# The low parts of the down phases' operands, split between VectorE and GpSimd

## The chip, the cores and the metric

The kernel runs on one core of one Trainium2 chip. The metric is device time of one execution in microseconds (us), lower is better. The engines named below are TensorE (PE in the profile: matmuls; PEld: its weight loads), VectorE (DVE), ScalarE (ACT), GpSimd (POOL) and SyncE (SP, which here issues all DMAs). SBUF is the on-chip memory that they share, PSUM the one that TensorE writes.

## The reference, cut to what matters

One layer over 1024 latent tokens and 256 context tokens, 1024 features wide, all in fp32:

```
x += 1/2 * gate1 * SwiGLU_1(mod(RMSNorm(x)))      # D_FF = 2816, context tokens too
x += gate2 * W_out [ Retention || ChunkGMLP ](mod(RMSNorm(x)) W_in)
x += 1/2 * gate3 * SwiGLU_2(mod(RMSNorm(x)))
return rmsnorm(x, final_g)

def swiglu(h, w1, w2):
    gate, up = jnp.split(h @ w1, 2, axis=-1)
    return (jax.nn.silu(gate) * up) @ w2          # this last product is the "down" one
```

The change is in the last line, the down product of each of the two SwiGLUs for the latent tokens.

## The kernel before

**Operands in two parts.** A matmul in full fp32 is made of three in the type fp32r. ScalarE copies an operand `raw` into fp32r (its high part), another engine computes the low part `raw - high`, and TensorE adds high x high, high x low and low x high in PSUM (L2186, L2187, L2188 for the down product).

**The down phase.** The down product uses Strassen's scheme in Winograd's form: 7 products (`NM`) of half size, each over 11 tiles (`HALF`) of the 2816 hidden features, so 77 steps (`STEPS`). One step has four groups of three matmuls with 512 columns. Its operands are one tile of tokens (128 x 512, gated activations or sums of them) and one of weights (128 x 512), which SyncE loads from HBM into a ring of six slots (`SLOTS`, L274 to L279). A slot is raw[:, 0, :] for tokens and raw[:, 1, :] for weights. Per step, in this order:

- SyncE: `load_step` (L634), as soon as the step six earlier is done on TensorE (`s_step`).
- ScalarE: `ring_high` (L1048), one copy of 128 x 1024, counted by `s_rh`.
- VectorE: `ring_low` (L1620), one subtraction of 128 x 1024, counted by `s_rl`.
- TensorE: `down_step` (L2190) waits for `s_rl`.

Between the steps each engine has further duties at written-out places, given by functions of the step (`mixer_opening` in the first feed-forward, `final_downs`, `final_squares` and `final_sum` in the second): VectorE adds finished products to the stream (`down_added`), sums parts of the modulation (`latent_sums`, L1449), and prepares the context's norm (`norm_mean(1, 0)` behind step 31, `norm_diagonal(1, 0)` behind step 32). TensorE sums that norm's squares behind step 26 and spreads its scale with `norm_scale(1, 0)` behind step 29 (L2006), for which it needs VectorE's diagonal DG (L1326), which needs GpSimd's reciprocal root RS (`norm_rsqrt`, L749).

**GpSimd's order.** Nothing reorders instructions: each engine runs its list as written, and a wait holds up all that stands behind it. Before a down phase stand the 22 blocks of the gate and up products. For the last of them, block 21, `gated_sums` (L778) makes three operations (L786, L788, L795) on the gated activations that VectorE has just finished (L1613, L1618). Behind the first phase's blocks GpSimd has `norm_rsqrt(1, 0)`, the low parts of the mixer's first two weight units (`low(0)`, `low(1)`, L743, 128 x 2048 each), and eight low parts of context tokens (HCL, L846). Behind the second's it has ten additions of squares for the final norm (L906, L911). During the steps it has nothing else to do.

Of the kernel before, what the change touches and what calls it, by code (L numbers as in the profile page):

```python
# [8 lines left out]
ALU = mybir.AluOpType  # L9
# [135 lines left out]
def layer(nc, x, ctx, c2, ada_units, w_units, w2_units, b_ada, norm_g, final_g, decay, ws, bs, cosine, sine, consts, powers, ident, out):  # L145
# [10 lines left out]
    with stack:  # L156
# [214 lines left out]
        s_w2st = sem("down_weight_sums_stored")  # L371
        s_ring = [sem(f"down_operands_loaded{r}") for r in range(NSLOT)]
        s_rh = sem("down_operands_high_done")
        s_rl = sem("down_operands_low_done")
        s_step = sem("down_step_done")
        s_sqt = sem("final_squares_done")
        s_qt = [sem(f"final_squares_added{t}") for t in range(2)]
        s_out = sem("stored")


# [353 lines left out]
        def _(pool):  # L734
# [25 lines left out]
                    pool.tensor_tensor(tokens(hl, b)(k), modulated_tile(place, b, k), tokens(hh, b)(k).bitcast(F32),  # L760
                                       ALU.subtract).then_inc(s_hl, 1)

            def feed_forward(f):
                s_wh, s_wl, s_fp = BS[f].wh, BS[f].wl, BS[f].fp

                def low_part(slot, src, count):
                    pool.wait_ge(s_wh, count)
                    pool.tensor_tensor(WVL[:, slot], src, WVH[:, slot].bitcast(F32), ALU.subtract).then_inc(s_wl, 1)

                def weight_low(g, m, raw=None):  # L770
                    low_part(weight_slot(f, g, m), weight_block(m, raw), weights_done(f, g, m))

                def token_low(v, k):
                    high, low = token_block((3, 2, 4, 5)[v], k)
                    pool.wait_ge(s_vh[v], 4 * f + k + 1)
                    pool.tensor_tensor(low, token_sum(v)[:, k, :], high.bitcast(F32), ALU.subtract).then_inc(s_vl[v], 1)

                def gated_sums(g):  # L778

                    h = HB[g % 2]  # L780
                    first, second = h[:, 0:TB], h[:, TB:SEQ]
                    for t in range(2):
                        pool.wait_ge(s_fp[t], g + 1)
                    if g >= HALF:
                        pool.wait_ge(s_trl, 16 * (HALF * f + g - HALF + 1))
                        pool.tensor_tensor(TBF[:, 0, :], first, TBF[:, 0, :], ALU.subtract).then_inc(s_ts, 1)  # L786
                        pool.wait_ge(s_ts, sums_done(f, g) - 2)
                        pool.tensor_tensor(TBF[:, 1, :], TBF[:, 0, :], TBF[:, 1, :], ALU.add).then_inc(s_ts, 1)  # L788
                        pool.wait_ge(s_ts, sums_done(f, g) - 1)
                    if f or g:  # L790
                        pool.wait_ge(s_tst, sums_stored(f, g - 1))
                    if g < HALF:
                        pool.tensor_tensor(TBF[:, 2, :], first, second, ALU.subtract).then_inc(s_ts, 1)
                    else:
                        pool.tensor_tensor(TBF[:, 2, :], second, TBF[:, 1, :], ALU.subtract).then_inc(s_ts, 1)  # L795

                def weight_pair_sums(j):

                    pool.wait_ge(s_w2, 48 * (HALF * f + j + 1))
                    n = SUMS * f + 4 * j  # L800
                    a11, a21, a12, s3, a22 = (WB[:, i, :] for i in range(5))
                    pool.tensor_tensor(s3, a11, a21, ALU.subtract).then_inc(s_w2s, 1)
                    pool.wait_ge(s_w2s, n + 1)
                    pool.tensor_tensor(a21, a21, a22, ALU.add).then_inc(s_w2s, 1)
                    pool.wait_ge(s_w2s, n + 2)
                    pool.tensor_tensor(a11, a21, a11, ALU.subtract).then_inc(s_w2s, 1)
                    pool.wait_ge(s_w2s, n + 3)
                    pool.tensor_tensor(a12, a12, a11, ALU.subtract).then_inc(s_w2s, 1)

                if f:  # L810
                    for n, slot in enumerate(DIRECT):
                        low_part(slot, direct_block(n), n + 1)
                    for m in ORDER1[:3]:
                        weight_low(1, m, RAW1)
                    norm_rsqrt(2, 2)
                    norm_low(2, 2, 0, 4)
                    pool.wait_ge(s_wl, weights_done(f, 1, 3))
                    for m in ORDER1[5:]:
                        weight_low(1, m, RAW1)
                else:  # L820
                    weight_low(1, 0)
                    pool.wait_ge(s_yb, NF)
                    for m in ORDER[1:]:
                        weight_low(1, m)
                for k in range(4):
                    token_low(3, k)
                for g in range(NF):
                    gated_sums(g)
                    if 1 <= g <= HALF:
                        weight_pair_sums(g - 1)  # L830

            pool.wait_ge(s_negh, 1)
            norm_rsqrt(0, 0)
            norm_low(0, 0)
            norm_rsqrt(0, 1)
            norm_rsqrt(0, 2)
            feed_forward(0)
            norm_rsqrt(1, 0)
            pool.wait_ge(s_w2st, 16 * HALF)
            pool.wait_ge(s_col, ADA_STEPS[0])  # L840
            pool.wait_ge(s_tst, sums_stored(0, NF - 1))
            low(0)
            low(1)
            for k in range(KT):
                pool.wait_ge(s_hh, 8 * J[1, 0] + k + 1)
                pool.tensor_tensor(HCL[:, k, :], XC[:, k, :], HCH[:, k, :].bitcast(F32), ALU.subtract).then_inc(s_hl, 1)  # L846
            norm_rsqrt(1, 1)
            norm_low(1, 1, 0, 4)
            norm_low(1, 1, 4, KT)
# [28 lines left out]
            for n, (i, name, a, b) in enumerate(FILLS):  # L878
# [19 lines left out]
                    norm_rsqrt(2, 1)  # L898
                if (name, a, b) in (("out", 1, 2), ("out", 1, 3)):
                    norm_low(2, 1, 4 * (b - 2), 4 * (b - 1))  # L900
            feed_forward(1)
            for n in range(1, 4):
                pool.wait_ge(s_sqt, n + 1)
                if n > 1:
                    pool.wait_ge(s_qt[1], n - 1)
                pool.tensor_tensor(SQT[1][:, 0, 0:TB], SQT[1][:, 0, 0:TB], SQT[1][:, n, 0:TB], ALU.add).then_inc(s_qt[1], 1)  # L906
            for n in range(1, KT):
                pool.wait_ge(s_sqt, 4 + n + 1)
                if n > 1:
                    pool.wait_ge(s_qt[0], n - 1)  # L910
                pool.tensor_tensor(SQT[0][:, 4, 0:TB], SQT[0][:, 4, 0:TB], SQT[0][:, (4 + n) % KT, 0:TB],  # L911
                                   ALU.add).then_inc(s_qt[0], 1)
            for b in (1, 2):
                norm_rsqrt(3, b)

# [375 lines left out]
        def _(dve):  # L1291
# [266 lines left out]
            def feed_forward(f, at_step):  # L1558
# [61 lines left out]
                def ring_low(s):  # L1620
                    raw, low_part, high_part = SLOTS[s % NSLOT]
                    dve.wait_ge(s_rh, STEPS * f + s + 1)
                    dve.tensor_tensor(low_part, raw, high_part.bitcast(F32), ALU.subtract).then_inc(s_rl, 1)  # L1623

                def block_period(g, q):
                    a = ADA_PERIODS.get(g) if f == 0 else None
# [356 lines left out]
        def _(pe):  # L1983
# [147 lines left out]
            def feed_forward(f, at_step, at_tile):  # L2131
# [58 lines left out]
                def down_step(s):  # L2190
                    i, j = divmod(s, HALF)
                    pe.wait_ge(s_rl, STEPS * f + s + 1)
                    for d in range(4):
                        if j == 0 and i >= 2:
                            pe.wait_ge(s_fyd, 4 * (i - 2) + d + 1)
                        ins = step_tile(s, d)
                    ins.then_inc(s_step, 1)

                def down_product():
                    if f:  # L2200
                        pe.wait_ge(s_xm, 8 * (J[2, 2] + 1))
                    pe.wait_ge(s_fp[1], 1)
                    pe.wait_ge(s_mods, N_ADA if f else ADA_STEPS[0])
                    for s in range(STEPS - MAJOR):
                        if s == HALF:
                            pe.wait_ge(s_c11, NF - 1)
                            pe.wait_ge(s_c12, NF - 1)
                            pe.wait_ge(s_c22, NF - 1)
                            pe.wait_ge(s_g1, NF)
                        if s == 3 * HALF and f == 0:  # L2210
                            pe.wait_ge(s_xm, 8 * (J[1, 0] + 1))
                        down_step(s)
                        at_step(s)
                    for d in range(4):
                        for s in range(STEPS - MAJOR, STEPS):
                            if d == 0:
                                pe.wait_ge(s_rl, STEPS * f + s + 1)
                            ins = step_tile(s, d)
                        ins.then_inc(s_step, 1)
                        at_tile(d)  # L2220
# [189 lines left out]
            def final_sum(s):  # L2410
                if s == STEPS - MAJOR - 1:
                    pe.wait_ge(BS[1].fyd, 24)
                    square_sum(0, 4, (s_qt[0], KT - 1), first=True).then_inc(s_st, 1)

            def final_norm(d):
                if d == 1:
                    norm_scale(3, 1)
                if d == 2:
                    pe.wait_ge(s_ms, J[3, 1] + 1)
                    square_sum(1, 0, (s_qt[1], 3), first=True)  # L2420
                    square_sum(1, 4, (s_sqt, 13))
                if d == 3:
                    for k in range(5, KT):
# [86 lines left out]
```

## Time and profile before

| what | us |
|---|---|
| median of 3 runs (lowest to highest) | 2052.42 (2052.02 to 2053.18) |
| profiled execution | 2052.53 |
| its span | 2050.7 |
| TensorE busy (L2186 to L2188 are the down phases) | 2008.0, 98% |
| VectorE busy | 1266.6, 62% |
| ScalarE busy | 758.9, 37% |
| GpSimd busy | 496.3, 24% |
| low parts of the ring on VectorE (L1623), 154 | 99.7 + 102.7 |

The first down phase begins at 688.5 us of the span, the second at 1821.1. An engine's busy time says how much it works, not whether another waits for it; idle time counts only where TensorE, which is busy almost throughout, waits. A matmul's reported duration (0.39 us) overlaps the next one's, so their pace is read from their starts.

### The profile page before, as it was taken

What the parts mean: (1) busy time and instruction counts of PE and PEld (TensorE: products, weight loads), DVE (VectorE), ACT (ScalarE), POOL (GpSimd) and SP (SyncE); (2) the same over time, 40 slices, a digit from 0 to 9 for tenths busy, and PEclk for the clock granted to TensorE, in tenths of its full rate; (3) what the DMA queues carried; (4) which work ended last, traced back from release to release, by engine and by line L of the source; (5) the groups of instructions that cost most, each with busy time, mean ns of one, the idle gap of its engine ahead of it and who ended that gap; (6) DMA issues with size and microseconds to landing.
All of it is one profiled execution on the core that took longest, in us unless ns stands there. A gap on an engine that the chain in (4) does not pass through costs nothing.

```text
span 2050.7 us, 26021 instructions
## 1 busy us (share of the span) xinstructions
PE 2008.0 (98%) x10112; PEld 1689.4 (82%) x10112; DVE 1266.6 (62%) x1887; ACT 758.9 (37%) x1098; POOL 496.3 (24%) x311
## 2 busy tenths in 40 slices
PE   7999999999999998999999999999999999999997
PEld 5999988888888887888989898877788888888886
DVE  5988666556788678775454324468656555555555
ACT  4333533333333354445121221446333333334342
POOL 1000042333221103014222222554332421210001
PEclk9999999999999999999999999999999999999998
DMA  8964436666656786733101011121656644466664
GB/s 335 353 258 145 143 106 204 214 205 206 215 186 215 256 297 196 258 112 109 42 21 42 31 43 61 62 82 57 212 198 206 213 161 151 161 212 192 191 194 154
DMA packets 108762, 343.52 MB, mean 168 GB/s; under 512 B 11488, under 2 KB 20960, under 8 KB 90464
## 3 DMA queue, kind: packets, MB, share of 16 engines
q1 hardware_dynamic: 108640, 341.85, 49.1%
q8 instruction: 81, 1.33, 0.3%
q14 instruction: 41, 0.34, 0.1%
HBM read 267.36 MB, written 74.45 MB: 167 GB/s over the span
## 4 chain that ended last, share of the span: by engine, by line
PE 85%; issue 5%; DVE 5%; ACT 2%; DMA 1%; POOL 1%; DVEq 0%; POOLq 0%; SPq 0%; ACTq 0%
PE PS L2144 12%; PE PS L2146 12%; PE PS L2145 12%; PE PS L1986 8%; PE PS L1988 8%; PE PS L1987 8%; PE PS L2186 5%; PE PS L2188 5%; PE PS L2187 5%; PE PS L2102 4%; DVE WVL L1577 1%; PE PS L2362 1%; DMA WR<-w_units 1%; PE PS L2043 1%; PE PS L2023 0%
## 5 line engine op out<-in xcount | busy, mean ns | idle before, releaser
L2144 PE MATMUL PS<-HH,WVH 128*128 128x512 f32 x672 | 265.8, 395 | 0.0
L2146 PE MATMUL PS<-HH,WVL 128*128 128x512 f32 x672 | 263.7, 392 | 0.0
L2145 PE MATMUL PS<-HL,WVH 128*128 128x512 f32 x672 | 261.9, 390 | 0.0
L1986 PE MATMUL PS<-HH,WH 128*128 128x512 f32 x416 | 165.0, 397 | 2.9 <-DVE WL L1768 2.9
L1988 PE MATMUL PS<-HH,WL 128*128 128x512 f32 x416 | 162.0, 389 | 0.0
L1987 PE MATMUL PS<-HL,WH 128*128 128x512 f32 x416 | 161.9, 389 | 0.0
L1577 DVE TENSOR_TENSOR WVL<-WR,WVH 128x512 fp32r<-128x512 f32 x160 | 115.1, 720 | 72.3 <-ACT WVH L1004 72.3
L2146 PEld LDWEIGHTS PS<-HH,WVL 128*128 128x128 f32 x672 | 126.1, 188 | 29.9
L2145 PEld LDWEIGHTS PS<-HL,WVH 128*128 128x128 f32 x672 | 126.2, 188 | 27.8
L2144 PEld LDWEIGHTS PS<-HH,WVH 128*128 128x128 f32 x672 | 126.3, 188 | 26.5
L1623 DVE TENSOR_TENSOR DLOW<-DRAW,DHIGH 128x1024 fp32r<-128x1024 f32 x78 | 99.7, 1286 | 71.3 <-ACT DHIGH L1052 70.9
L1623 DVE TENSOR_TENSOR HL<-HLF,HH 128x1024 fp32r<-128x1024 f32 x76 | 102.7, 1361 | 61.1 <-ACT HH L1052 60.6
L1004 ACT ACTIVATE WVH<-WR 128x512 fp32r<-128x512 f32 x164 | 98.1, 623 | 96.2 <-PE PS L2146 80.3
L743 POOL TENSOR_TENSOR WL<-WR,WH 128x2048 fp32r<-128x2048 f32 x20 | 92.2, 4612 | 166.4 <-ACT WH L921 166.4
L1052 ACT ACTIVATE DHIGH<-DRAW 128x1024 fp32r<-128x1024 f32 x78 | 82.5, 1060 | 124.8 <-DMA DRAW<-down_weight_sums 73.8
L2186 PE MATMUL PS<-DHIGH 128*128 128x512 f32 x312 | 124.2, 398 | 0.0
L921 ACT ACTIVATE WH<-WR 128x2048 fp32r<-128x2048 f32 x47 | 89.6, 1906 | 90.0 <-PE PS L1988 90.0
L2187 PE MATMUL PS<-DLOW,DHIGH 128*128 128x512 f32 x312 | 122.7, 393 | 0.0
L2188 PE MATMUL PS<-DHIGH,DLOW 128*128 128x512 f32 x312 | 122.4, 392 | 0.0
L749 POOL TENSOR_TENSOR RS<-MS,NEGH 128x4 f32<-128x4 f32 (+3 forms) x16 | 22.9, 1434 | 404.9 <-DVE MS L1323 347.0
L1004 ACT ACTIVATE WVH<-ST 128x512 fp32r<-128x512 f32 x125 | 78.7, 631 | 111.1 <-PE PS L2146 66.1
L2186 PE MATMUL PS<-HH 128*128 128x512 f32 x304 | 119.4, 393 | 0.1
(282 smaller groups left out, 4974.5 us busy)
## 6 DMA issues: line engine op xcount, KB each, us to landing
WR<-w_units SPq DMA_DIRECT2D x89, 1024.0 KB, 5.8
gated<-HB SPq DMA_DIRECT2D x44, 512.0 KB, 6.6
down_weight_sums<-WB SPq DMA_DIRECT2D x22, 1024.0 KB, 3.8
gated_sums<-TBF SPq DMA_DIRECT2D x22, 768.0 KB, 4.1
AW<-ada_units SPq DMA_DIRECT2D x12, 1024.0 KB, 13.2
HLF<-down_weight_sums SPq DMA_DIRECT2D x46, 256.0 KB, 3.4
W2RB<-w_units SPq DMA_DIRECT2D x22, 512.0 KB, 3.6
WB<-w_units SPq DMA_DIRECT2D x22, 512.0 KB, 3.6
```

Source lines behind the costliest of these rows:

```text
L1004: act.activation(WVH[:, slot], src, ACT.Copy).then_inc(s_wh, 1)
L1577: dve.tensor_tensor(WVL[:, m], weight_block(m), WVH[:, m].bitcast(F32), ALU.subtract).then_inc(s_wl, 1)
L1623: dve.tensor_tensor(low_part, raw, high_part.bitcast(F32), ALU.subtract).then_inc(s_rl, 1)
L1986: pe.matmul(dst, wh, xh, start=first, stop=False)
L1987: pe.matmul(dst, wh, xl, start=False, stop=False)
L1988: return pe.matmul(dst, wl, xh, start=False, stop=last)
L2144: pe.matmul(bank[:, :], wh, xh, start=first, stop=False, skip_group_check=True)
L2145: pe.matmul(bank[:, :], wh, xl, start=False, stop=False, skip_group_check=True)
L2146: ins = pe.matmul(bank[:, :], wl, xh, start=False, stop=k == 3, skip_group_check=True)
L2186: pe.matmul(bank[:, :], wh, xh, start=j == 0 and i in (0, 1, 3), stop=False, skip_group_check=True)
L2187: pe.matmul(bank[:, :], wh, xl, start=False, stop=False, skip_group_check=True)
L2188: return pe.matmul(bank[:, :], wl, xh, start=False, stop=j == HALF - 1, skip_group_check=True)
```

## The change

The low part of a step is made by two engines. VectorE subtracts the tokens' half alone (128 x 512), GpSimd the weights' half (128 x 512, a new semaphore `s_rlw`), and TensorE waits for both. GpSimd's loop over the 77 steps stands behind its loop over the blocks. What GpSimd did behind the blocks is now done at fixed steps: in the first phase `norm_rsqrt(1, 0)` behind step 31, `low(0)` behind 36, `low(1)` behind 40, one context tile behind each of 46 to 53; in the second the additions of squares behind 32 to 34, 65 to 67 and 72 to 75. These additions are counted by one semaphore instead of two.

```diff
         s_rh = sem("down_operands_high_done")
-        s_rl = sem("down_operands_low_done")
+        s_rl = sem("down_tokens_low_done")
+        s_rlw = sem("down_weights_low_done")
...
-            def feed_forward(f):
+            def feed_forward(f, at_step):
...
                     gated_sums(g)
                     if 1 <= g <= HALF:
                         weight_pair_sums(g - 1)
+                for s in range(STEPS):
+                    raw, low_part, high_part = SLOTS[s % NSLOT]
+                    pool.wait_ge(s_rh, STEPS * f + s + 1)
+                    pool.tensor_tensor(low_part[:, 1, :], raw[:, 1, :], high_part[:, 1, :].bitcast(F32),
+                                       ALU.subtract).then_inc(s_rlw, 1)
+                    at_step(s)
...
-            feed_forward(0)
-            norm_rsqrt(1, 0)
-            pool.wait_ge(s_w2st, 16 * HALF)
-            pool.wait_ge(s_col, ADA_STEPS[0])
-            pool.wait_ge(s_tst, sums_stored(0, NF - 1))
-            low(0)
-            low(1)
-            for k in range(KT):
-                pool.wait_ge(s_hh, 8 * J[1, 0] + k + 1)
-                pool.tensor_tensor(HCL[:, k, :], XC[:, k, :], HCH[:, k, :].bitcast(F32), ALU.subtract).then_inc(s_hl, 1)
+            def mixer_opening(s):
+                if s == 31:
+                    norm_rsqrt(1, 0)
+                if s == 36:
+                    pool.wait_ge(s_w2st, 16 * HALF)
+                    pool.wait_ge(s_tst, sums_stored(0, NF - 1))
+                    pool.wait_ge(s_col, ADA_STEPS[0])
+                    low(0)
+                if s == 40:
+                    low(1)
+                if 46 <= s < 54:
+                    k = s - 46
+                    pool.wait_ge(s_hh, 8 * J[1, 0] + k + 1)
+                    pool.tensor_tensor(HCL[:, k, :], XC[:, k, :], HCH[:, k, :].bitcast(F32), ALU.subtract).then_inc(s_hl, 1)
+
+            feed_forward(0, mixer_opening)
...
-            feed_forward(1)
-            for n in range(1, 4):
-                pool.wait_ge(s_sqt, n + 1)
...
+            def final_squares(s):
+                if 32 <= s < 35:
+                    n = s - 31
+                    pool.wait_ge(s_sqt, n + 1)
...
+                for n in range(1, KT):
+                    if s == (64 + n if n < 4 else 68 + n):
+                        pool.wait_ge(s_sqt, 4 + n + 1)
...
+            feed_forward(1, final_squares)
...
                 def ring_low(s):
                     raw, low_part, high_part = SLOTS[s % NSLOT]
                     dve.wait_ge(s_rh, STEPS * f + s + 1)
-                    dve.tensor_tensor(low_part, raw, high_part.bitcast(F32), ALU.subtract).then_inc(s_rl, 1)
+                    dve.tensor_tensor(low_part[:, 0, :], raw[:, 0, :], high_part[:, 0, :].bitcast(F32), ALU.subtract).then_inc(s_rl, 1)
...
                 def down_step(s):
                     i, j = divmod(s, HALF)
                     pe.wait_ge(s_rl, STEPS * f + s + 1)
+                    pe.wait_ge(s_rlw, STEPS * f + s + 1)
```

Lines of the changed file are 1 higher up to the blocks on GpSimd and 17 higher from VectorE's feed-forward on: GpSimd's L786 is L787 there, TensorE's L2186 is L2203. GpSimd's new operation is L835.

GpSimd before, from the last block of the first feed-forward on (TBF holds the gated sums, RS the reciprocal roots, WL and HCL low parts, DLOW and HL those of the ring; in brackets the semaphores waited for):

```order
L786 TENSOR_TENSOR TBF<-HB_146,TBF 128x512 [waits first_gated_reloaded,block0_gated_ready1,block0_gated_ready0]
L788 TENSOR_TENSOR TBF<-TBF 128x512 [waits gated_sums_done]
L795 TENSOR_TENSOR TBF<-HB_146,TBF 128x512 [waits gated_sums_stored,gated_sums_done]
L749 TENSOR_TENSOR RS<-MS,NEGH 128x2 [waits norm_mean_ready]
L743 TENSOR_TENSOR WL<-WR,WH 128x2048 [waits gated_sums_stored,unit_high_done,ada_columns_ready,down_weight_sums_stored]
L743 TENSOR_TENSOR WL<-WR,WH 128x2048 [waits unit_high_done]
L846 TENSOR_TENSOR HCL<-XC,HCH 128x256 [waits modulated_high_done] x8
```

GpSimd after, the same place, with the halves of the first six steps:

```order
L787 TENSOR_TENSOR TBF<-HB_146,TBF 128x512 [waits first_gated_reloaded,block0_gated_ready1,block0_gated_ready0]
L789 TENSOR_TENSOR TBF<-TBF 128x512 [waits gated_sums_done]
L796 TENSOR_TENSOR TBF<-HB_146,TBF 128x512 [waits gated_sums_stored,gated_sums_done]
L835 TENSOR_TENSOR DLOW_169<-DRAW_168,DHIGH_170 128x512 [waits down_operands_high_done]
L835 TENSOR_TENSOR DLOW_172<-DRAW_171,DHIGH_173 128x512 [waits down_operands_high_done]
L835 TENSOR_TENSOR DLOW_175<-DRAW_174,DHIGH_176 128x512 [waits down_operands_high_done]
L835 TENSOR_TENSOR HL<-HLF,HH 128x512 [waits down_operands_high_done] x3
```

Where nothing stood between the gated sums and the rsqrt, the weights' halves of the steps now follow the gated sums.

GpSimd after, the middle of the first phase (halves of steps 30 and 31, then the rsqrt, and so on to step 41):

```order
L835 TENSOR_TENSOR DLOW_169<-DRAW_168,DHIGH_170 128x512 [waits down_operands_high_done]
L835 TENSOR_TENSOR DLOW_172<-DRAW_171,DHIGH_173 128x512 [waits down_operands_high_done]
L750 TENSOR_TENSOR RS<-MS,NEGH 128x2 [waits norm_mean_ready]
L835 TENSOR_TENSOR DLOW_175<-DRAW_174,DHIGH_176 128x512 [waits down_operands_high_done]
L835 TENSOR_TENSOR HL<-HLF,HH 128x512 [waits down_operands_high_done] x3
L835 TENSOR_TENSOR DLOW_169<-DRAW_168,DHIGH_170 128x512 [waits down_operands_high_done]
L744 TENSOR_TENSOR WL<-WR,WH 128x2048 [waits ada_columns_ready,unit_high_done,gated_sums_stored,down_weight_sums_stored]
L835 TENSOR_TENSOR DLOW_172<-DRAW_171,DHIGH_173 128x512 [waits down_operands_high_done]
L835 TENSOR_TENSOR DLOW_175<-DRAW_174,DHIGH_176 128x512 [waits down_operands_high_done]
L835 TENSOR_TENSOR HL<-HLF,HH 128x512 [waits down_operands_high_done] x2
L744 TENSOR_TENSOR WL<-WR,WH 128x2048 [waits unit_high_done]
L835 TENSOR_TENSOR HL<-HLF,HH 128x512 [waits down_operands_high_done]
```

The two large low parts stood directly behind the rsqrt before; now five steps' halves are between the rsqrt and the first of them, and four between the two.

## Rows read from the trace of the kernel before

**Rows 1.** The page, part 1: busy time, share of the span, instructions
```profile
PE 2008.0 (98%) x10112; PEld 1689.4 (82%) x10112; DVE 1266.6 (62%) x1887; ACT 758.9 (37%) x1098; POOL 496.3 (24%) x311
```

**Rows 2.** TensorE's waits: releaser, us in total, times, longest us
```profile
PE PS L2006 <- DVE DG L1326: 9.0, 3, 5.7
PE PS L1986 <- DVE WL L1768: 2.9, 2, 2.7
```

**Rows 3.** Timeline, first phase's head: start us, us, instruction [idle before <-releaser]
```profile
688.53 0.39 PE L2186 MATMUL PS<-DHIGH 128*128 128x512 f32 x1
689.36 0.69 DVE L1618 TENSOR_TENSOR HB<-HB,SG 128x512 f32<-128x512 f32 x1 [0.45 <-ACT SG L1046]
...
690.13 1.30 POOL L786 TENSOR_TENSOR TBF<-HB,TBF 128x512 f32<-128x512 f32 x1 [14.94 <-DVE HB L1618]
...
690.31 2.20 DVE L1623 TENSOR_TENSOR DLOW<-DRAW,DHIGH 128x1024 fp32r<-128x1024 f32 x1 [0.26 <-ACT DHIGH L1052]
691.51 2.15 POOL L788 TENSOR_TENSOR TBF<-TBF 128x512 f32<-128x512 f32 x1
693.74 2.16 POOL L795 TENSOR_TENSOR TBF<-HB,TBF 128x512 f32<-128x512 f32 x1
```

**Rows 4.** Timeline, second phase's head
```profile
1821.07 0.39 PE L2186 MATMUL PS<-DHIGH 128*128 128x512 f32 x1
...
1822.67 1.30 POOL L786 TENSOR_TENSOR TBF<-HB,TBF 128x512 f32<-128x512 f32 x1 [14.68 <-DVE HB L1618]
```

**Rows 5.** Timeline, middle of the first phase
```profile
767.67 1.06 ACT L1052 ACTIVATE DHIGH<-DRAW 128x1024 fp32r<-128x1024 f32 x1 [4.26 <-DMA DRAW<-down_weight_sums]
768.96 1.07 ACT L1052 ACTIVATE DHIGH<-DRAW 128x1024 fp32r<-128x1024 f32 x1 [0.23 <-DMA DRAW<-down_weight_sums]
...
770.14 1.71 POOL L749 TENSOR_TENSOR RS<-MS,NEGH 128x2 f32<-128x2 f32 x1 [74.24 <-DVE MS L1323]
771.82 9.19 POOL L743 TENSOR_TENSOR WL<-WR,WH 128x2048 fp32r<-128x2048 f32 x2
771.88 4.73 DVE L1326 TENSOR_TENSOR DG<-ID,RS 128x256 f32<-128x256 f32 x1 [0.60 <-POOL RS L749]
...
776.66 1.22 PE L2006 MATMUL PS<-DG,ONES 128*128 128x256 f32 x2 [5.68 <-DVE DG L1326]
...
777.33 0.99 PE L2186 MATMUL PS<-DHIGH 128*128 128x512 f32 x1
...
781.09 0.39 PE L2188 MATMUL PS<-DHIGH,DLOW 128*128 128x512 f32 x1
```

**Rows 6.** Windows: stretch, its us, busy time (count) by engine, PEclk, DMA, GB/s
```profile
777.00:781.00 4.00, 4.00 (x10) 3.14 (x10) 4.00 (x1) 0.00 (x0) 4.00 (x1) 0.50 0.02 4
946.60:950.00 3.40, 3.40 (x15) 2.84 (x16) 1.70 (x3) 2.80 (x5) 2.34 (x2) 1.00 0.67 217
```

**Rows 7.** Lines L1449, L1341: count, duration ns min/median/max, first and last start
```profile
L1449 DVE SCALAR_TENSOR_TENSOR ASB<-AWB,CS,ASB x56: 470/485/1408, 532.7 to 677.6; 128x256 f32<-128x256 f32 x56
...
L1341 DVE TENSOR_TENSOR HF<-X,PS x16: 674/680/689, 911.3 to 947.6; 128x512 f32<-128x512 f32 x16
```

**Rows 8.** Timeline, steps 36 and 37; then groups: busy us, mean ns | idle
```profile
788.54 1.06 ACT L1052 ACTIVATE DHIGH<-DRAW 128x1024 fp32r<-128x1024 f32 x1 [0.83 <-DMA DRAW<-down_weight_sums]
...
796.07 0.39 PE L2186 MATMUL PS<-DHIGH 128*128 128x512 f32 x1
...
798.80 0.39 PE L2186 MATMUL PS<-DHIGH 128*128 128x512 f32 x1
...
L743 POOL TENSOR_TENSOR WL<-WR,WH 128x2048 fp32r<-128x2048 f32 x20 | 92.2, 4612 | 166.4 <-ACT WH L921 166.4
...
L846 POOL TENSOR_TENSOR HCL<-XC,HCH 128x256 fp32r<-128x256 f32 x8 | 8.9, 1152 | 19.3 <-ACT HCH L1166 19.3
```

**Rows 9.** Timeline, end of the second phase
```profile
2004.09 8.52 POOL L911 TENSOR_TENSOR HHF<-HHF 128x512 f32<-128x512 f32 x4 [16.42 <-ACT HHF L1273]
...
2021.25 0.16 DVE L1323 TENSOR_SCALAR MS<-PS 128x4 f32<-128x4 f32 x1 [0.64 <-PE PS L2127]
```

More of the change, by code:

```diff
@@ L373, in layer @@
         s_rh = sem("down_operands_high_done")
-        s_rl = sem("down_operands_low_done")
+        s_rl = sem("down_tokens_low_done")
+        s_rlw = sem("down_weights_low_done")
         s_step = sem("down_step_done")
         s_sqt = sem("final_squares_done")
-        s_qt = [sem(f"final_squares_added{t}") for t in range(2)]
+        s_qt = sem("final_squares_added")
         s_out = sem("stored")
@@ L900, in _ @@
                     norm_low(2, 1, 4 * (b - 2), 4 * (b - 1))
-            feed_forward(1)
-            for n in range(1, 4):
-                pool.wait_ge(s_sqt, n + 1)
[L904 to L912, printed above, removed]
+            def final_squares(s):
+                if 32 <= s < 35:
+                    n = s - 31
+                    pool.wait_ge(s_sqt, n + 1)
+                    if n > 1:
+                        pool.wait_ge(s_qt, n - 1)
+                    pool.tensor_tensor(SQT[1][:, 0, 0:TB], SQT[1][:, 0, 0:TB], SQT[1][:, n, 0:TB], ALU.add).then_inc(s_qt, 1)
+                for n in range(1, KT):
+                    if s == (64 + n if n < 4 else 68 + n):
+                        pool.wait_ge(s_sqt, 4 + n + 1)
+                        if n > 1:
+                            pool.wait_ge(s_qt, 3 + n - 1)
+                        pool.tensor_tensor(SQT[0][:, 4, 0:TB], SQT[0][:, 4, 0:TB], SQT[0][:, (4 + n) % KT, 0:TB],
+                                           ALU.add).then_inc(s_qt, 1)
+            feed_forward(1, final_squares)
             for b in (1, 2):
@@ L2217, in down_product @@
                                 pe.wait_ge(s_rl, STEPS * f + s + 1)
+                                pe.wait_ge(s_rlw, STEPS * f + s + 1)
                             ins = step_tile(s, d)
@@ L2412, in final_sum @@
                     pe.wait_ge(BS[1].fyd, 24)
-                    square_sum(0, 4, (s_qt[0], KT - 1), first=True).then_inc(s_st, 1)
+                    square_sum(0, 4, (s_qt, 3 + KT - 1), first=True).then_inc(s_st, 1)
             def final_norm(d):
@@ L2419, in final_norm @@
                     pe.wait_ge(s_ms, J[3, 1] + 1)
-                    square_sum(1, 0, (s_qt[1], 3), first=True)
+                    square_sum(1, 0, (s_qt, 3), first=True)
                     square_sum(1, 4, (s_sqt, 13))
```

## The prediction, made before the change was run

> **What bounds the kernel now.** I read the page first: TensorE (PE) is busy 98% of the span, every other engine 62% or less [rows 1]. Work taken off VectorE is therefore worth nothing by itself. What counts is where TensorE stands still, so the next view was its waits: the longest entry is norm scaling (L2006) waiting for the diagonal that VectorE builds, 9.0 us in three waits, one of 5.7 us [rows 2]. Nothing in that list belongs to the matmuls of the down phases (L2186 to L2188). There are two of these phases, one for each feed-forward, of 77 steps each, and TensorE starts a new step every 2.72 us (796.07 to 798.80 with 12 matmuls, 0.227 us apart) [rows 8]. The timeline then showed three places on which the change acts: the heads of the two phases [rows 3, 4] and the middle of the first one [rows 5].
>
> **Part 1, the new wait at the head of each phase.** Each step now waits for two low parts: the tokens' half from VectorE and the weights' half from GpSimd. GpSimd reaches its first half only after the last three subtractions and additions of gated_sums(21), because the loop over the steps stands behind that call, as the order rows on GpSimd show. These three can't start earlier than today. The first waits for VectorE's last gating product (L1618), which runs at 689.36, released by ScalarE's silu of TensorE's last product. It starts at 690.13, while TensorE starts step 0 at 688.53 [rows 3]. So the first weights' half comes late by construction. How late:
>
> Where a VectorE operation with both inputs in SBUF meets a GpSimd one, they take turns. GpSimd's L786 ends at 691.43, and only then does VectorE's low part from 690.31 finish, at 692.51, 1.08 us later. GpSimd's L788 ends at 693.66, 1.15 us after that [rows 3]. Alone, L786 takes 1.30. With tokens' halves VectorE's turn is half as long, 0.55 (half of 1.08). The chain: L786 ends at 691.43, VectorE 691.98, L788 693.13, VectorE 693.68, L795 694.83, VectorE 695.38, first weights' half 696.53, TensorE some 0.1 later at 696.6. Against 688.53 that is a stall of 8.1 us. Bounds: without any turn of VectorE, four GpSimd operations of 1.30 with gaps of 0.08 end at 695.6, a stall of 7.1; with L795 ending at 695.90 as now and one more turn of VectorE, of whole size, it is 695.90 + 1.08 + 1.15 = 698.1, a stall of 9.6. I take 8.1, because L788 and L795 take 2.15 and 2.16 today, so VectorE has a low part ready at each turn. The second phase has the same distance between TensorE's first step and GpSimd's L786: 1822.67 less 1821.07, against 690.13 less 688.53, both 1.60 [rows 3, 4]. Twice 8.1 makes 16.2.
>
> In the trace a GpSimd operation starts 0.08 us after the one before it ends (691.43 to 691.51 [rows 3]). The Trainium skill (Perfetto Trace Analysis, GPSIMD Engine Instruction) says that the reported span of a GpSimd instruction is unreliable and start-to-start spacing should be used. By that rule each of three links is 0.08 longer where VectorE doesn't cover it, and the two stalls together would be up to 0.5 longer; by the spans they are as above.
>
> What stands behind the wait on TensorE is the whole rest of the phase, and the loads of slots wait for its steps, so nothing runs on meanwhile. After it, GpSimd finishes a half every 1.3 to 1.85 us against a step of 2.72, so the second and later steps don't wait.
>
> **Part 2, the clock after the stall.** After today's pause of 5.68 us TensorE resumes at the lower level: the granted clock is 0.50 (1.2 GHz) from 777 to 781 [rows 6]. Nine matmul starts from 777.33 to 781.09 take 3.76 us instead of 9 x 0.227 = 2.04 [rows 5], a loss of 1.7. A pause of 8.1 us should bring at least that; bounds 0 and 3.4 (twice the row) each. I take 1.7 twice, 3.4.
>
> **Part 3, the middle of the first phase.** Today GpSimd is idle in the phase but for norm_rsqrt(1,0), and right behind it stand the two low parts of the mixer's first weights. These start at 771.82 and hold GpSimd for 9.19 us in two pieces. The diagonal, at 771.88 on VectorE, takes 4.73 us instead of a fraction of one, and TensorE waits for it from 770.98 to 776.66: 5.68, and 1.7 more at the low clock, 7.4 in all [rows 5]. In the changed order a weights' half of one step stands behind the rsqrt and the first large low part comes five steps later. New chain: high part 31 is ready at 768.7 and 32 at 770.0; the weights' half 31, one turn of VectorE, then the rsqrt, which took 1.71 beside VectorE's work: about 772.1. GpSimd then starts half 32 at once, as it did today with L743, 0.05 us ahead of the diagonal, which is so held for one GpSimd operation of some 1.25, ending near 773.6. TensorE would wait 773.7 less 770.98 = 2.7. I take no low clock behind a pause that short: behind TensorE's wait of 2.7 us at L1986 [rows 2], which ends at 946.6, the granted clock is 1.00 (2.4 GHz) [rows 6]. Gain 7.4 less 2.7 = 4.7. Bounds: 7.4 (the diagonal not held and early) and 0 (something large is in front again).
>
> **Part 4, the moved duties.** They must fit into the room between high part and use. VectorE's half per step, about 0.55, and GpSimd's, 1.15 to 1.30, take turns: some 1.85 of 2.72 us. At step 37 the high part ends at 789.60 and TensorE starts the step at 798.80: 9.2 us [rows 8]. A large low part (L743, mean 4.61) ahead of such a half leaves some 2 to 3, since two of VectorE's turns and the halves themselves come on top; the second one, at step 40, finds less room, as GpSimd has just caught up. The eight context low parts of steps 46 to 53 (L846, mean 1.15) make 1.15 + 1.30 + 0.55 = 3.0 per step against 2.72, so they eat 8 x 0.3 = 2.4 of the room. Cost taken 0, and up to 4 us if loads land late there. VectorE's adds from PSUM don't take part: L1341 with one input in PSUM stays at 674 to 689 ns, while L1449, with both in SBUF, goes from 485 to 1408 beside GpSimd [rows 7]. At the end of the second phase the last four squares are now added one behind each of the halves 72 to 75. They took 8.52 us in a row, ending at 2012.61; VectorE's mean that waits for their sum on TensorE was at 2021.25 [rows 9]. The last add would now end near 2020, when TensorE wants it: 0 to 0.5, taken as 0.2. VectorE's shorter halves free 77 x 2 x 0.55 = 85 us of an engine that no down step waits for: 0.
>
> **Sum.** 16.2 + 3.4 - 4.7 + 0.2 = 15.1. The profiled execution took 2052.53 (span 2050.7 and 1.8 around it), the median of the runs is 2052.42, so both give 2067.6.
>
> **Rivals.**
> A, the room in the middle gives out (14%): the two large low parts and the context low parts make steps 37 to 54 wait as well. For it: the exchange with VectorE and loads that land late in the first phase. Against: 9.2 us of room at step 37. Price 4 more: 2071.6. The Trainium skill (Perfetto Trace Analysis, Optimizing Scalar/DVE Operations) warns that moving work between GpSimd and VectorE may not help because they share a port; the turns in rows 3 agree, and A is what it would come to if they didn't fit in a step.
> B, the middle isn't mended (10%): the diagonal still waits as long behind other GpSimd work or a late load. No gain: 2052.4 + 16.2 + 3.4 + 0.2 = 2072.2.
> C, the heads are cheap and the middle is mended in full (8%): stalls of 7.1, no low clock behind them, all of 7.4 back: 14.2 - 7.4 = 6.8, so 2059.2.
> D, not slower (6%): the first head's delay is absorbed. If TensorE's later waits were for work that doesn't hang on its own steps, they would shrink by what it comes late, and the 9.8 us of the first head (8.1 + 1.7) would vanish in them. Then the 9.8 of the second head stand against the middle's 7.4 and the other two waits of L2006, 9.0 - 5.7 = 3.3 [rows 2], of which half may go: 9.8 - 7.4 - 1.7 = +0.7, so 2053.2, and faster than before if all 3.3 go. It decides once about 8 us of the first head are absorbed. Against: the diagonals' sums come from TensorE's own matmuls, so these waits move with it.
>
> **How the numbers follow.** The forecast has 62%. A measurement can tell 0.2%, 4.1 us. Everything but D is slower by more than that; D is split into same and faster. The range leaves out D and the outer ends of C and B: its low end is 2061, between C and the forecast with a low clock of nothing at the heads (2064.2); its high end is 2074, the sum with stalls of 9.6 and the rest as taken is 2070.6, plus most of A. Chances: faster 0.03, same 0.03, slower 0.94.
>
> **What would show it.** TensorE's waits gain an entry, L2203 on GpSimd's weights' half (L835), of two times and about 8 us each, with gated_sums' three operations running meanwhile; the granted clock falls just behind each; the wait of L2006 on the diagonal drops from 5.7 to about 3, with one half of 1.3 us between rsqrt and diagonal on GpSimd; steps 37 to 54 start 2.72 apart. I'm wrong if L2203 waits less than 5 us, if it waits at many steps, or if the middle is as long as before.

## The result, and the profile after

| | before | changed |
|---|---|---|
| median, us (lowest to highest, runs) | 2052.74 (2052.02 to 2053.18, 4) | 2074.08 (2072.60 to 2075.23, 4) |
| profiled execution / its span | 2052.53 / 2050.7 | 2073.66 / 2071.9 |
| GpSimd busy | 496.3 | 739.0 |
| VectorE busy | 1266.6 | 1244.8 |

The change makes the kernel slower by 21.3 us: ratio 1.0103, 95% interval 1.0087 to 1.0119. The forecast was 2067.6 in a range of 2061 to 2074; 2074.08 lies at its very edge, and of the four runs two are below 2074 and two above.

TensorE's waits in the changed kernel (who waits, for whom, us in total, times, longest), against [rows 2]:

```profile
PE PS L2203 <- POOL DLOW L835: 16.5, 2, 8.6
...
PE PS L2023 <- DVE DG L1343: 5.3, 3, 2.1
```

The new entry has two waits, one at each head. The wait for the diagonal, 9.0 in total before, is down to 5.3. The timeline of the first head (start, us, instruction, idle before and releaser), to be held against [rows 3]:

```profile
690.34 0.69 DVE L1635 TENSOR_TENSOR HB<-HB,SG 128x512 f32<-128x512 f32 x1 [1.31 <-ACT SG L1063]
...
691.11 1.27 POOL L787 TENSOR_TENSOR TBF<-HB,TBF 128x512 f32<-128x512 f32 x1 [14.94 <-DVE HB L1635]
...
691.28 1.65 DVE L1640 TENSOR_TENSOR DLOW<-DRAW,DHIGH 128x512 fp32r<-128x512 f32 x1 [0.25 <-ACT DHIGH L1069]
...
692.46 1.60 POOL L789 TENSOR_TENSOR TBF<-TBF 128x512 f32<-128x512 f32 x1
...
694.13 1.59 POOL L796 TENSOR_TENSOR TBF<-HB,TBF 128x512 f32<-128x512 f32 x1
695.69 4.63 POOL L835 TENSOR_TENSOR DLOW<-DRAW,DHIGH 128x512 fp32r<-128x512 f32 x3
...
697.54 0.77 PE L2203 MATMUL PS<-DHIGH 128*128 128x512 f32 x1 [7.87 <-POOL DLOW L835]
```

GpSimd works from 691.11 on with gaps of 0.08 at most. The first of L835's three takes 1.71 and ends at 697.40, and TensorE starts step 0 at 697.54. L789 and L796 take 1.60 each where they took 2.15 and 2.16: VectorE's turn is half as long, as its form is now 128 x 512.

The timeline of the middle of the first phase, against [rows 5]:

```profile
781.48 1.16 POOL L750 TENSOR_TENSOR RS<-MS,NEGH 128x2 f32<-128x2 f32 x1
782.62 1.26 POOL L835 TENSOR_TENSOR DLOW<-DRAW,DHIGH 128x512 fp32r<-128x512 f32 x1
...
782.67 1.49 DVE L1343 TENSOR_TENSOR DG<-ID,RS 128x256 f32<-128x256 f32 x1 [0.60 <-POOL RS L750]
...
784.21 0.70 PE L2023 MATMUL PS<-DG,ONES 128*128 128x256 f32 x2 [1.97 <-DVE DG L1343]
```

The diagonal starts 0.05 behind a GpSimd half and ends only after it, but that half takes 1.26, where the large low part of the kernel before took 4.50. TensorE's pause is 1.97 where it was 5.68, and no low clock follows.

Where the 21.2 us between the two spans arise can be read from the starts of TensorE's steps in the two timelines (shift of the changed kernel against the one before):

| stretch | added, us | forecast |
|---|---|---|
| up to the first head | +0.97 | 0 |
| wait at the first head (step 0 at 688.53 and 697.54, less 0.97) | +8.04 | +8.1 |
| step 0 to 1 at the low clock (2.72 and 4.32) | +1.60 | +1.7 |
| steps 1 to 29 | +0.65 | 0 |
| steps 29 to 31, the diagonal and the clock behind it | -5.78 | -4.7 |
| steps 31 to 72 | +2.53 | 0 |
| from there to the second head | +1.65 | 0 |
| wait at the second head | +8.75 | +8.1 |
| low clock behind it | +2.30 | +1.7 |
| the rest (with 0.65 behind step 72 of the second phase) | +0.50 | +0.2 |

Two of the unforeseen entries, the steps 1 to 29 and 31 to 72, are one matter: TensorE waits for VectorE's half, not GpSimd's, at four steps: 23, 40, 43 and 67. Three of these waits, in the timeline of TensorE (that at step 43 is 0.22):

```profile
762.42 0.50 PE L2203 MATMUL PS<-HH 128*128 128x512 f32 x1 [0.33 <-DVE HL L1640]
...
812.99 0.50 PE L2203 MATMUL PS<-HH 128*128 128x512 f32 x1 [0.49 <-DVE HL L1640]
...
888.52 0.50 PE L2203 MATMUL PS<-DHIGH 128*128 128x512 f32 x1 [1.04 <-DVE DLOW L1640]
```

and, in the timeline, what VectorE and GpSimd did ahead of the first of them:

```profile
755.12 5.55 DVE L1330 TENSOR_TENSOR ACC<-ACC,SQ 128x256 f32<-128x256 f32 x7
760.59 1.77 DVE L1640 TENSOR_TENSOR HL<-HLF,HH 128x512 fp32r<-128x512 f32 x1
...
757.64 1.30 POOL L835 TENSOR_TENSOR HL<-HLF,HH 128x512 fp32r<-128x512 f32 x1 [4.24 <-ACT HH L1069]
758.93 2.89 POOL L835 TENSOR_TENSOR DLOW<-DRAW,DHIGH 128x512 fp32r<-128x512 f32 x2
```

VectorE adds the context's squares behind step 22. Seven additions of two SBUF inputs would need some 3.7 us (the first start 0.53 apart, while GpSimd is idle), and take 5.55. The last two of them take 1.45 and 1.34 instead of 0.43, as GpSimd's halves of steps 23 and 24 run beside them, and step 23's tokens' half, which stands behind all of them, takes 1.77 instead of 0.68 beside the next one. At step 67 it is the same with the latent tokens' squares. At step 40 it is the second large low part, as the timelines of VectorE and GpSimd show:

```profile
807.83 5.11 DVE L1640 TENSOR_TENSOR HL<-HLF,HH 128x512 fp32r<-128x512 f32 x1
...
807.32 5.07 POOL L744 TENSOR_TENSOR WL<-WR,WH 128x2048 fp32r<-128x2048 f32 x1
```

By step starts, steps 1 to 29 and 66 to 68 add 2.0 us by the first cause, steps 37 to 54 1.3 us by the second and its sequel: at step 43 VectorE's three products of `latent_sums`, held for 1.4 each by GpSimd's halves, stand ahead of its own half.

### The profile page after: what moved, and what is told of

Its sections match the earlier page's. It is cut to its first block, busy times and chain, and to the rows that moved or that the text cites. A ratio compares the mean times of both kernels' runs of the same rounds, so it can differ in the third digit from the quotient of the medians.

```text
span 2071.9 us, 26319 instructions
## 1 busy us (share of the span) xinstructions
PE 2013.9 (97%) x10112; PEld 1691.0 (82%) x10112; DVE 1244.8 (60%) x1887; ACT 759.4 (37%) x1098; POOL 739.0 (36%) x465
## 4 chain that ended last, share of the span: by engine, by line
PE 83%; DVE 7%; ACT 3%; issue 2%; DMA 2%; POOL 2%; SPq 0%; DVEq 0%; POOLq 0%; ACTq 0%
PE PS L2161 12%; PE PS L2163 12%; PE PS L2162 12%; PE PS L2003 8%; PE PS L2005 8%; PE PS L2004 8%; PE PS L2203 5%; PE PS L2205 5%; PE PS L2204 5%; PE PS L2119 4%; DVE WVL L1594 1%; PE PS L2381 1%; DVE HHF L1466 1%; PE PS L2060 1%; DMA WR<-w_units 1%
## 5 line engine op out<-in xcount | busy, mean ns | idle before, releaser
L2161 PE MATMUL PS<-HH,WVH 128*128 128x512 f32 x672 | 265.8, 396 | 0.0
L835 POOL TENSOR_TENSOR DLOW<-DRAW,DHIGH 128x512 fp32r<-128x512 f32 x78 | 128.4, 1653 | 71.8 <-ACT DHIGH L1069 71.5
L2161 PEld LDWEIGHTS PS<-HH,WVH 128*128 128x128 f32 x672 | 126.3, 188 | 26.5 <-ACT U L1053 0.2
L835 POOL TENSOR_TENSOR HL<-HLF,HH 128x512 fp32r<-128x512 f32 x76 | 122.7, 1622 | 64.3 <-ACT HH L1069 64.2
L787 POOL TENSOR_TENSOR TBF<-HB,TBF 128x512 f32<-128x512 f32 x22 | 29.1, 1325 | 321.3 <-DVE HB L1635 306.2
L2203 PE MATMUL PS<-DHIGH 128*128 128x512 f32 x312 | 125.7, 403 | 17.7 <-POOL DLOW L835 16.5
L1640 DVE TENSOR_TENSOR DLOW<-DRAW,DHIGH 128x512 fp32r<-128x512 f32 x78 | 73.5, 948 | 104.5 <-ACT DHIGH L1069 104.5
L1640 DVE TENSOR_TENSOR HL<-HLF,HH 128x512 fp32r<-128x512 f32 x76 | 81.1, 1081 | 68.7 <-ACT HH L1069 68.7
```

The source lines that it names most:

```text
L835: pool.tensor_tensor(low_part[:, 1, :], raw[:, 1, :], high_part[:, 1, :].bitcast(F32), ALU.subtract).then_inc(s_rlw, 1)
L1640: dve.tensor_tensor(low_part[:, 0, :], raw[:, 0, :], high_part[:, 0, :].bitcast(F32), ALU.subtract).then_inc(s_rl, 1)
L2161: pe.matmul(bank[:, :], wh, xh, start=first, stop=False, skip_group_check=True)
L2203: pe.matmul(bank[:, :], wh, xh, start=j == 0 and i in (0, 1, 3), stop=False, skip_group_check=True)
```

## The experiments

Four kernels first, one part of the matter each. A ratio is to runs of the kernel before that were made beside the kernel in question: a median of 2052.61 for these four, of 2051.48 for the last four.

**e1_early6**: the place of the first halves in GpSimd's list.

```diff
                 for g in range(NF):
+                    if g == NF - 1:
+                        for s in range(6):
+                            weights_half(s)
                     gated_sums(g)
...
-                for s in range(STEPS):
+                for s in range(6, STEPS):
```

> The changed kernel, but GpSimd makes the weights' halves of steps 0 to 5 ahead of gated_sums(21) instead of behind it. Theory 1 (place in GpSimd's list): both heads' waits of 7.9 and 8.6 us and the low clock behind them (1.6 and 2.3) go, so 2074.1 - 8.0 - 8.75 - 3.9 = about 2053.4, and about 3 us of short waits inside the first phase stay. Rival (the exchange between GpSimd and VectorE is what costs): moving six halves changes little, 2070 or more.

Measured: 2055.22 us (2051.12 to 2059.24, 10 runs), ratio to before 1.0012 (1.0001 to 1.0023). That is 1.8 above what was expected, but some 19 of the 21 us go with nothing moved but six halves. In the view of waits, TensorE's for GpSimd's halves fall from 16.5 to

```profile
PE PS L2209 <- POOL DLOW L831: 2.2, 2, 1.1
```

and these two are at step 8, not at step 0. They have a cause of their own, which SyncE's timeline shows:

```profile
696.09 0.43 SPq L648 DMA_DIRECT2D DRAW<-w_units  x1
703.26 0.32 SPq L603 DMA_DIRECT2D gated_sums<-TBF  x1
703.62 0.43 SPq L648 DMA_DIRECT2D DRAW<-gated  x1
```

SyncE stores the gated sums ahead of load 8. With six halves in front, gated_sums(21) ends at 703.2, and the loads stand behind that store. So the order of the two jobs matters on two queues.

**e2_lows_later**: the middle alone, with no split.

```diff
             norm_rsqrt(1, 0)
+            pool.wait_ge(s_rh, 37)
...
             low(0)
+            pool.wait_ge(s_rh, 41)
             low(1)
```

> The kernel before, with no split: only GpSimd's two large low parts behind the rsqrt are held until the high parts of steps 36 and 40 are done. Theory 1: the diagonal is no longer behind a large GpSimd operation, TensorE's wait there falls from 5.7 us to about 1.3 and the low clock behind it goes, so -6: about 2046.5. The large low parts later cost nothing, as VectorE makes both halves itself and has 5 us or more of room. Rival: a low part held for 4.6 us at step 36 or 40 makes TensorE wait there, and the gain is 3 or less (2049.5 or more).

Measured: 2046.84 us (2044.65 to 2048.80, 7 runs), ratio 0.9974 (0.9963 to 0.9986): faster than both kernels, as forecast to 0.3 us. (Its profiled execution, 2044.65, is the fastest of the seven, so the traces of the two kernels differ by 7.9 and not by 5.8.) The diagonal and TensorE's wait for it, in its timeline:

```profile
772.95 0.43 DVE L1328 TENSOR_TENSOR DG<-ID,RS 128x256 f32<-128x256 f32 x1 [0.60 <-POOL RS L749]
...
773.43 0.70 PE L2008 MATMUL PS<-DG,ONES 128*128 128x256 f32 x2 [1.39 <-DVE DG L1328]
```

With nothing of GpSimd's beside it the diagonal takes 0.43, against 4.73 [rows 5] and 1.49 in the changed kernel. None of the waits at steps 23, 40, 43 and 67 is there. For 23 and 67 the split is needed; at step 40 it is not, as e5_scale_30 below shows.

**e3_pause**: a pause by itself, with no split.

```diff
                     for s in range(STEPS - MAJOR):
+                        if s == 0:
+                            pe.wait_ge(s_ts, sums_done(f, NF - 1))
```

> The kernel before, with no split: TensorE alone waits at step 0 of each down phase until the three operations of gated_sums(21) are done. It prices a pause by itself. Theory 1: 695.9 - 688.5 = 7.4 us of pause in each phase and 1.7 to 2.3 of low clock behind each, 18 to 19 in all: 2071. Rival (a pause at a head is taken up later, or the clock is not what costs): 2067 or less.

Measured: 2075.37 us (2072.76 to 2076.67, 4 runs), ratio 1.0108 (1.0093 to 1.0123), 4 more than expected. The pauses, in the view of waits:

```profile
PE PS L2186 <- POOL TBF L795: 16.0, 2, 8.6
```

7.4 and 8.6, not twice 7.4: in the second phase the pause is longer than in the first here too. The low clock behind them costs 1.9 and 2.5 (steps 0 to 1 of 4.65 and 5.26 instead of 2.72). With 0.3 more to step 2 of the second phase the two heads make 21.1 of the 24.0 us between the two spans. The rest is a balance of things that lie elsewhere: 1.5 us are there by 46 us of the span, where nothing differs, and low clock falls behind other pauses than in the kernel before. Behind the wait at L1986, 2.64 long, this kernel has it (the row of windows below) and the one before has not [rows 6]:

```profile
952.00:958.00 6.00, 3.36 (x9) 2.60 (x9) 4.08 (x4) 4.31 (x7) 3.17 (x2) 0.67 0.40 123
```

Thirteen of its next starts are 0.427 apart instead of 0.227, some 2.9 us in all with the first. Behind the wait of 1.21 us at L1996 it is the other way round. The windows there, of the kernel before and of this one:

```profile
923.40:928.00 4.60, 4.60 (x26) 4.60 (x27) 3.18 (x11) 3.05 (x3) 3.52 (x3) 0.63 0.70 241
...
933.10:937.70 4.60, 4.60 (x39) 4.60 (x40) 3.17 (x11) 3.06 (x3) 3.54 (x3) 1.00 0.64 228
```

That is 1.4 us which the kernel before pays and this one doesn't. So the rival is refuted, a pause at the head isn't taken up by anything, and whether the low clock follows a pause of 1.2 to 2.7 us differs from kernel to kernel.

**e4_second_only**: the split and the additions' new places in the second phase alone; `feed_forward(0)` and what follows it as before. GpSimd makes no half in the first phase, and VectorE makes both there:

```diff
-                for s in range(STEPS):
+                for s in range(STEPS if f else 0):
...
+                    part = slice(0, 1 if f else 2)
```

> The split in the second down phase alone, with the squares' additions at their new places; the first phase and its GpSimd duties as before. Theory 1: the second head's 8.75 + 2.3 and some 0.4 at the tail, +11.4: 2064.2; no short waits inside the phase, since VectorE has few other operations there. Rival (the exchange costs throughout a phase): over 2066, with waits of L2186's successor spread over the steps.

Measured: 2062.92 us (2061.98 to 2063.88, 4 runs), ratio 1.0049 (1.0034 to 1.0064): +10.3 where +11.4 was expected. The one wait in the view of waits that is new:

```profile
PE PS L2199 <- POOL DLOW L835: 7.9, 1, 7.9
```

On top come 2.5 of low clock to step 1, 0.3 to step 2, and 0.5 at the tail. No step in between waits: the second phase has few two-input operations on VectorE, and taking turns alone costs nothing there.

Then four that follow from these.

**e5_scale_30**: e2_lows_later, and the scale behind step 30.

```diff
-                if s == 29:
+                if s == 30:
                     norm_scale(1, 0)
```

> e2_lows_later, and TensorE spreads the context's norm scale behind step 30 instead of 29. It still waited 1.4 us for the diagonal at step 29 there; one step more is 2.7 us. Theory 1: that wait goes and no other comes, since VectorE reads the scale only at step 34: 2046.8 - 1.5 = 2045.3. Rival: the scale is later, so VectorE's context products (L1753) end later and TensorE waits for them at step 33: no gain, 2046.8.

Measured: 2045.50 us (2043.23 to 2050.79, 12 runs), ratio 0.9974 (0.9965 to 0.9983). In the view of waits the diagonal's has 3.4 us in two, after 4.7 in three in e2_lows_later; that of the middle is gone:

```profile
PE PS L2008 <- DVE DG L1328: 3.4, 2, 2.1
```

But the ratio is that of e2_lows_later, and as the runs of the kernel before beside it were about 1 us faster too (2051.48 against 2052.61), the expected 1.5 can't be told from nothing. One wait of 0.5 us for VectorE's low part (at step 40) came in return, behind the second large low part on GpSimd; steps 39 to 46 take 1.1 us more than in e2_lows_later. So without any split, too, VectorE's low part can be late there.

**e6_early2**: as e1_early6, with two halves instead of six ahead of gated_sums(21).

> The changed kernel with only the halves of steps 0 and 1 ahead of gated_sums(21). Theory 1 (place in the list): the half of step 2 now ends near 695.5 to 696.5 by the turns, against 694.0 at which TensorE wants it, so each head waits 1.5 to 2.5 us at step 2, with or without a low clock: 2055.2 to 2060, between e1_early6 and the changed kernel, with the wait at step 2 and not at step 0. Rival (how much is moved doesn't set the wait): as the changed kernel, 2074, or as e1_early6.

Measured: 2062.54 us (2061.89 to 2064.57, 4 runs), ratio 1.0058 (1.0045 to 1.0071). The wait is at step 2 of each phase, as expected, but the time is above the 2055 to 2060. The view of waits:

```profile
PE PS L2209 <- POOL DLOW L831: 7.0, 2, 3.8
```

GpSimd's timeline at the first head:

```profile
690.77 1.84 POOL L787 TENSOR_TENSOR TBF<-HB,TBF 128x512 f32<-128x512 f32 x1 [1.69 <-DMA TBF<-gated]
692.69 1.62 POOL L789 TENSOR_TENSOR TBF<-TBF 128x512 f32<-128x512 f32 x1
694.39 1.59 POOL L796 TENSOR_TENSOR TBF<-HB,TBF 128x512 f32<-128x512 f32 x1
695.95 1.70 POOL L831 TENSOR_TENSOR DLOW<-DRAW,DHIGH 128x512 fp32r<-128x512 f32 x1
```

All four operations have to wait their turn here, L787 too (1.84 instead of 1.27), so the half ends at 697.65 and not at 695.5 to 696.5. Behind the second of the waits, 3.8 us long, TensorE loses another 1.7 to the low clock; behind the first, 3.2 long, it loses 0.1, and the windows there have the full clock:

```profile
697.79:701.00 3.21, 3.21 (x14) 2.66 (x15) 0.85 (x1) 0.77 (x1) 3.21 (x3) 1.00 1.02 368
```

Another 2.8 come in behind step 72 of the second phase: a wait of 1.0 for the last square on GpSimd (L932), with low clock behind it. The wait moves with the place of the halves in the list and its size follows the chain of turns.

**e7_between**: two halves ahead, one behind each of gated_sums(21)'s first two operations.

```diff
                         pool.tensor_tensor(TBF[:, 0, :], first, TBF[:, 0, :], ALU.subtract).then_inc(s_ts, 1)
+                        if g == NF - 1:
+                            weights_half(2)
...
                         pool.tensor_tensor(TBF[:, 1, :], TBF[:, 0, :], TBF[:, 1, :], ALU.add).then_inc(s_ts, 1)
+                        if g == NF - 1:
+                            weights_half(3)
```

> The changed kernel with the halves of steps 0 and 1 ahead of gated_sums(21) and those of steps 2 and 3 between its three operations. Theory 1: GpSimd has at most one other operation between two halves, so neither step 2 nor step 8 waits (1.1 and 1.0 us in e1_early6): 2053, about as the kernel before, as the mended middle pays for the short waits inside the first phase and the tail. Rival: the heads wait again (over 2056), because two GpSimd operations and a turn of VectorE, 3.1 us, are more than a step of 2.72.

Measured: 2052.61 us (2049.34 to 2057.35, 10 runs), ratio 1.0006 (0.9997 to 1.0015): no difference from the kernel before. GpSimd's halves in TensorE's view of waits:

```profile
PE PS L2213 <- POOL HL L835: 1.4, 4, 0.4
```

Three of these four waits, 0.4 us each, are at steps 3 and 4, the fourth at step 41; by step starts the heads still cost 0.7 and 1.5 us of 9.6 and 11.1. What the split then still has over e2_lows_later, 0.3%, lies there, in the steps 40 to 46 (1.1), at the tail (0.6), and in the diagonal, for which TensorE waits 2.7 us here with low clock behind it, and 1.4 there without (2.9).

**e8_spread**: VectorE's bursts of additions spread over steps.

```diff
-                if s == 22:
-                    add_squares(1, 0)
+                if 22 <= s < 26:
+                    for k in (2 * (s - 22), 2 * (s - 22) + 1):
+                        add_square(1, 0, k)
...
-                if s == 66:
-                    for k in range(4):
-                        add_square(1, 1, k)
+                if 66 <= s < 70:
+                    add_square(1, 1, s - 66)
```

> The changed kernel with VectorE's additions of squares spread: the context's two behind each of steps 22 to 25 instead of eight behind 22, the latent ones' first four one behind each of 66 to 69 instead of four behind 66. Theory (a burst of two-input additions on VectorE, each held by a GpSimd half, makes the tokens' half of the next step late): the waits at steps 23 (0.5 us) and 67 (1.2 us) go, the heads and the rest stay, about 2072.4. Rival (the loads that land late there cause them): both waits stay.

Measured: 2070.02 us, one run. The steps 23 and 67 no longer wait, those at 40 and 43 still do; the first phase's steps 31 to 72 add 1.1 us instead of 2.5. Waits for VectorE's halves (1.3 and 0.8 in the changed kernel) are down, in the view of waits, to

```profile
PE PS L2203 <- DVE HL L1640: 0.4, 1, 0.4
PE PS L2203 <- DVE DLOW L1640: 0.2, 1, 0.2
```

Some 0.5 us came in at steps 26 and 27, where TensorE sums the squares that are now later. So the bursts were the cause at steps 23 and 67, not late loads. The time itself, from a single run and 2.4 below what was expected, is no more than in line: this profile also has no low clock behind the wait at L2161 (1.6 us) and a second head 0.7 shorter.

## Why the prediction was right, and what it missed

**Part 1, the wait at the heads: right.** 8.04 and 8.75 against 8.1 twice. The chain of turns gave the first half's end as 696.53; without the 0.97 by which everything was late it was 696.4 (695.69 + 1.71 - 0.97). The chain was made of reported ends and durations. The Trainium skill (Perfetto Trace Analysis, GPSIMD Engine Instruction) says that the reported span of a GpSimd instruction is unreliable and that such times don't compose; in this trace they did, to 0.1 us. e1_early6 shows the cause by undoing the order alone, e6_early2 by moving the wait to step 2. The second head was 0.7 longer than the first. The prediction took both as the same from their same distance of 1.60 [rows 3, 4]; in the changed kernel's timeline GpSimd's first operation there is released by a reload from HBM, 0.4 later, and takes 1.61 instead of 1.27:

```profile
1832.72 1.61 POOL L787 TENSOR_TENSOR TBF<-HB,TBF 128x512 f32<-128x512 f32 x1 [15.06 <-DMA TBF<-gated]
```

In e4_second_only and e8_spread VectorE releases it, it takes 1.26 and 1.27, and the second head waits 7.9.

**Part 2, the clock behind the pause: right in kind, a little small.** 1.60 and 2.30 against 1.7 each, and e3_pause and e4_second_only give 1.9, 2.5 and 2.5. The row of windows from step 0 of the second phase on has a granted clock of 0.50:

```profile
1839.40:1844.00 4.60, 4.52 (x11) 3.58 (x12) 0.00 (x0) 0.00 (x0) 4.60 (x4) 0.50 0.00 0
```

**Part 3, the middle: right mechanism, gain 1.1 larger.** 5.78 against 4.7. The half held the diagonal for 1.49 as foreseen, but the rsqrt took 1.16 and not 1.71, since VectorE's turn beside it is now short. That reason for the 1.16 is read from the two timelines and has no run of its own. The pause was 1.97 instead of 2.7; the other 0.4 of the 1.1 is low clock that the kernel before had beyond the 1.7 taken.

**Part 4, the moved duties: this term was mis-sized.** The text took it as 0 with up to 4; it was 0.65 + 2.53 = 3.2 in the first phase. The check was made for GpSimd only: whether its half has room behind a large low part. That held. What was late was VectorE's half, which the text had called free. Since each of VectorE's two-input operations can be held by a GpSimd operation, a burst of them behind one step takes longer by most of a GpSimd half for each half that falls into it. That is 2.0 of the 3.2; e8_spread removes it by spreading the burst, e2_lows_later by having no halves on GpSimd. The other 1.3 come behind the second large low part, which held VectorE's half of step 40 for 5.11 us; e8_spread leaves them as they are. (Steps 31 to 37 gained 0.1.) The steps 37 to 54, which were to start 2.72 apart, did so but for steps 39, 40, 42 and 43. At the tail the last addition (2040.13 + 1.28) was 0.4 us late for TensorE, within the 0 to 0.5 given.

**Outside the sum:** 0.97 ahead of the first head and 1.65 between the phases. The first has no part in the change: all of it is there by 46 us, where nothing was changed, and other profiles have between -0.3 (e5_scale_30) and 1.5 there (e4_second_only, whose first phase is that of before). Of the second the row of windows below shows most, a low clock behind a 2.0 us wait at L2161. Of the ten profiles only those of the kernel before and of e8_spread don't have it there. What decides it is open.

```profile
1458.50:1462.00 3.50, 3.50 (x9) 2.67 (x9) 2.19 (x4) 0.88 (x2) 0.00 (x0) 0.51 0.69 253
```

**The sum: 6 us too low, and inside the range by luck in part.** It gave 15.1 and the spans differ by 21.2. The difference is 3.2 of part 4, 2.6 outside the sum, 1.1 at the heads and 0.3 in the rest, less 1.1 in the middle. The range reached up to 2074 for other reasons, stalls of 9.6 each and most of rival A; neither came. The mechanism of the heads and of the middle is shown; that the number just held is not owed to it.

**The rivals.** A (room gives out, 2071.6) came true in part: its steps 37 to 54 cost 1.3 and not 4, by VectorE's half, not GpSimd's; the rest of part 4 lies outside these steps. B fell: the middle was mended. C fell: the heads cost in full. D fell, and e3_pause shows it best: nothing took up a pause.

## What to carry to other kernels

Where a new duty is put on an engine, ask first what stands in front of it in that engine's list at the moment when it is first needed; here that alone was 20 us, and six instructions moved ahead took 19 back. Then ask the same of every engine that shares something with it: halving an operation on VectorE doesn't free it if its partner now takes turns with everything that VectorE does from SBUF. And look at what a good part of a change does alone: only the two large low parts moved from behind the rsqrt were worth having (2046.8, ratio 0.9974), and the split gained nothing even with its heads mended (e7_between, ratio 1.0006).

## What the runs showed of the hardware

- A VectorE operation with two SBUF inputs and a GpSimd one on SBUF take turns whole, one operation each. The 128 x 256 diagonal took 0.43 us alone, 1.49 beside a half of 1.26 and 4.73 beside a large low part.
- The low clock (0.50, 1.2 GHz) followed each pause of TensorE of 7.4 us or more at the heads, and cost 1.6 to 2.9 us. Behind shorter pauses their length doesn't tell whether it comes. A clock of 0.50 followed 2.64 us at L1986 in e3_pause (some 2.9 us), one of 1.00 followed 2.65 us there in the kernel before and 3.21 us at step 2 in e6_early2, and behind 1.21 us at L1996 it was 0.63 in the kernel before and 1.00 in e3_pause. A difference of 2 to 3 us between two profiles can be this alone.
